# The order of the output quarters and input turns at the end of a stage

## The chip, the cores and the metric

The kernel runs on one core of a Trainium2 chip. The metric is the device time of one execution in microseconds (us); the median of three runs is 2865.96 us, with 2865.45 and 2866.62 at the ends.

## The reference

The program computes three transformer-like blocks one after the other on a residual `x` of 256 tokens x 1024 features in float32. It has ten gated feed-forward networks (width 2816), a gated delta rule, latent attention, a hybrid of a state-space model and block attention, a spatial gating unit and a pooling mixer. Cut to what matters here, each stage has this form:

```
x = x + 0.5 * ((silu(gate) * up) @ w_down)        # a feed-forward network
x = x + concat(mixed) @ w_out                     # a mixer
h = rms_norm(x, g)       or      x = layer_norm(alpha * x + ..., g, b)
```

So a stage ends with a product into the 256 x 1024 residual, and the next stage begins with that residual, turned (transposed) and normed, as input of its first product.

## The kernel before

Every product of float32 operands is made of three float32r matmuls: both operands are split in a rounded high part (`hi`, by ScalarE) and a rest (`lo`, by VectorE), and hi x hi, hi x lo and lo x hi are added in PSUM. Weights come by DMA from SyncE's queue into five slots. `load_weights` waits with `used` until TensorE has given a slot back; `round_weights` (L213) makes the high part on ScalarE, `split_weights` (L232) the rest on VectorE, at most three items ahead. Each engine works through its instructions in the order in which the program issues them, and waits on semaphores.

The output of a stage is 256 tokens x 1024 features, held in the four banks of `acc`. A quarter is 128 tokens x 512 features, one bank. `quarter` (L337) multiplies 256 rows of the weights (one item, here called a tile) into it: 2 x 3 matmuls of 512 columns. The output product goes over the rows in tiles, four quarters per tile. The last two tiles, n and n + 1, are done by `last_rows` (L353), which mixes their quarters. Quarter i of tile n + 1 completes the sum of quarter i of the output: the first three count up `quarters`, the last `used`. `before(j)` is the caller's hook ahead of the j-th step; for j = 0 and j = 2 it waits for the split of the operand of the one or the other tile (in the latent mixer, j = 1 also issues the last head's product).

When a quarter is complete, `add_quarter` (L376, on VectorE) adds it to `x` (L384 or L386). Then comes the tail of the stage, of one of two kinds:

- `FeedTail` (L523): the next stage's input is `x` as it is. `turn` (L413) transposes 128 x 512 elements by four matmuls (L421) into one of two banks of `work`; it waits for the addition of that quarter, and for turns 2 and 3 (counted from 0) also for the split of the turn two before. `round_quarter` (L431 without a gain, L436 with) runs on ScalarE, `split_quarter` (L446, L451) on VectorE. Turns 0 and 1 stand in `last_rows`, 2 and 3 in the next stage's first product (`before_chunk`, L506). VectorE's order is: additions 0 and 1, weight splits, input splits 0 and 1, additions 2 and 3, input splits 2 and 3, inverse root and diagonals (L473 to L477), weight splits. ScalarE's order is: weight rounding, input roundings 0 and 1, weight rounding, input roundings 2 and 3, squares (L463), root (L466). TensorE then sums the diagonals to a row (L491).
- `NormTail` (L566): the residual is normed first. All four turns stand in the next stage. VectorE's order is: weight splits, addition and statistics of the first two quarters, norm of the first 128 tokens (L632, L641), third addition, in the most cases the input splits 0 and 1, fourth addition, norm of the other tokens.

`last_rows` ends fourteen stages. The delta mixer (residual additions from 437 us) has its own order and does not call it.

| first addition, us | stage that ends | tail | input rounding |
|---|---|---|---|
| 223.87 | feed-forward | FeedTail | with gain |
| 626.38 | feed-forward | FeedTail | plain |
| 833.53 | feed-forward | FeedTail | plain |
| 922.23 | latent mixer | FeedTail | plain |
| 1105.13 | feed-forward | FeedTail | with gain |
| 1291.07 | feed-forward | NormTail | plain |
| 1721.71 | hybrid mixer's output | NormTail | plain |
| 1909.07 | feed-forward | NormTail | plain |
| 2095.82 | feed-forward | FeedTail | with gain |
| 2243.07 | gating mixer | FeedTail | plain |
| 2428.60 | feed-forward | FeedTail | plain |
| 2612.00 | feed-forward | FeedTail | with gain |
| 2671.50 | pooling mixer | FeedTail | plain |
| 2856.16 | feed-forward | NormTail | none, the output is stored |

Of the kernel before, what the change touches and what calls it, by code (L numbers as in the profile page):

```python
# [96 lines left out]
class Core:  # L97
# [255 lines left out]
    def last_rows(self, pe, n, pairs, tail, before):  # L353
        order = tail.order
        self.arrived(pe, n)
        for i in range(2):
            before(i)
            self.quarter(pe, n, pairs[0], order[i], False, False)
        self.arrived(pe, n + 1)
        for i in range(2):  # L360
            before(2 + i)
            self.quarter(pe, n + 1, pairs[1], order[i], False, True).then_inc(*self.quarters.up())
        before(4)
        self.quarter(pe, n, pairs[0], order[2], False, False)
        if tail.early:
            tail.feed.turn(pe, 0)
        before(5)
        self.quarter(pe, n, pairs[0], order[3], False, False).then_inc(self.used, 1)
        if tail.early:
            tail.feed.turn(pe, 1)  # L370
        before(6)
        self.quarter(pe, n + 1, pairs[1], order[2], False, True).then_inc(*self.quarters.up())
        before(7)
        self.quarter(pe, n + 1, pairs[1], order[3], False, True).then_inc(self.used, 1)

# [190 lines left out]
class NormTail:  # L566
    early = False
    order = BY_TOKENS
# [3269 lines left out]
```

## Time and profile before

| what | value |
|---|---|
| median of three runs | 2865.96 us |
| the profiled execution's own time | 2871.76 us |
| its span, first to last instruction | 2869.9 us |
| TensorE busy | 2784.2 us, 97% |
| VectorE busy | 1795.8 us, 63% |
| ScalarE busy | 1491.9 us, 52% |
| granted TensorE clock, mean | 0.994 |
| moved by DMA | 489.14 MB |

A matmul is shown with its modelled end, so neighbours overlap: the distance from one start to the next is what it costs. Idle time before an instruction is put down to the semaphore event that came last; "issue" is idle time for which the profile shows no releaser. Times in the rows count from the start of the span.

### The profile page before, as it was taken

The numbers are of one execution on the slowest core, as the hardware profiler recorded it, in microseconds if no ns is written. First come the engines' busy times: TensorE is split into PE (matmuls) and PEld (weight loads), VectorE is DVE, ScalarE is ACT, GpSimd is POOL, SyncE is SP. The second block draws the span as 40 slices with busy tenths as digits, with TensorE's granted clock in tenths as the row PEclk, the third lists the DMA queues.
The fourth block names the chain that finished last, engine by engine and source line by source line (L and its number), as shares of the span: only waits on it lengthen the run. The fifth ranks groups of instructions, "written<-read, shape, count | busy, mean of one in ns | idle before, by whom it ended". The sixth has DMA issues, their size and how long they took to land. (4 is left out here: it accounts for less than half of the span.)

```text
span 2869.9 us, 47489 instructions
## 1 busy us (share of the span) xinstructions
PE 2784.2 (97%) x20533; PEld 2599.5 (91%) x20533; DVE 1795.8 (63%) x2467; ACT 1491.9 (52%) x2011; POOL 26.5 (1%) x41
## 2 busy tenths in 40 slices
PE   7999999999999999999999999999999999999999
PEld 7998978999986999999998998989999899998898
DVE  5557756566666656555678656466656656656755
ACT  6447545455555555443575634445454555554653
POOL 1000000000000000000001000000000000000000
PEclk9999999999999999999999999999999999999999
DMA  6555115655652566665453455655565565564654
GB/s 227 191 177 163 59 45 176 191 181 180 195 165 80 186 194 207 193 191 165 144 179 104 133 175 192 192 176 191 191 191 176 167 194 192 183 195 158 198 191 132
DMA packets 370111, 489.14 MB, mean 170 GB/s; under 512 B 15424, under 2 KB 329186, under 8 KB 369776
## 3 DMA queue, kind: packets, MB, share of 16 engines
q1 hardware_dynamic: 368944, 485.90, 53.1%
q8 instruction: 162, 2.65, 0.4%
q14 instruction: 45, 0.37, 0.0%
q0 software_dynamic: 640, 0.20, 0.0%
q10 hardware_dynamic: 320, 0.01, 0.0%
HBM read 485.02 MB, written 1.05 MB: 169 GB/s over the span
## 5 line engine op out<-in xcount | busy, mean ns | idle before, releaser
L887 PE MATMUL work<-input_hi,weights_hi 128*128 128x256 f32 x3424 | 950.6, 278 | 1.9 <-DVE weights_lo L251 1.8
L889 PE MATMUL work<-input_lo,weights_hi 128*128 128x256 f32 x3424 | 947.0, 277 | 0.0
L890 PE MATMUL work<-input_hi,weights_lo 128*128 128x256 f32 x3424 | 946.7, 276 | 0.0
L241 DVE TENSOR_TENSOR weights_lo<-weights_raw,weights_hi 128x2048 fp32r<-128x2048 f32 (+2 forms) x282 | 629.4, 2235 | 321.4 <-ACT weights_hi L221 320.9
L887 PEld LDWEIGHTS work<-input_hi,weights_hi 128*128 128x128 f32 x3424 | 643.5, 188 | 3.0 <-DVE weights_lo L251 2.2
L889 PEld LDWEIGHTS work<-input_lo,weights_hi 128*128 128x128 f32 x3424 | 643.5, 188 | 0.2
L890 PEld LDWEIGHTS work<-input_hi,weights_lo 128*128 128x128 f32 x3424 | 643.1, 188 | 0.0
L225 ACT ACTIVATE weights_hi<-weights_raw,params 128x512 fp32r<-128x512 f32 (+2 forms) x736 | 462.0, 701 | 317.9 <-DMA weights_raw<-in_ffn_w_gu 157.6
L221 ACT ACTIVATE weights_hi<-weights_raw 128x2048 fp32r<-128x2048 f32 (+2 forms) x282 | 524.2, 1865 | 160.0 <-DMA weights_raw<-in_ffn_w_up 97.2
L251 DVE SCALAR_TENSOR_TENSOR weights_lo<-weights_raw,params,weights_hi 128x512 fp32r<-128x512 f32 (+2 forms) x736 | 492.4, 732 | 163.3 <-ACT weights_hi L225 163.2
L344 PE MATMUL acc<-weights_hi,hidden_hi 128*128 128x512 f32 x880 | 344.5, 392 | 2.9 <-ACT v_mla L2229 1.4
L349 PE MATMUL acc<-weights_hi,hidden_lo 128*128 128x512 f32 (+1 forms) x970 | 343.6, 370 | 0.0
L345 PE MATMUL acc<-weights_lo,hidden_hi 128*128 128x512 f32 x880 | 343.0, 390 | 0.0
L284 PE MATMUL work<-input_hi,weights_hi 128*128 128x256 f32 (+1 forms) x960 | 273.5, 285 | 4.2 <-DVE input_lo L451 2.2
L285 PE MATMUL work<-input_lo,weights_hi 128*128 128x256 f32 (+1 forms) x960 | 268.6, 280 | 0.0
L286 PE MATMUL work<-input_hi,weights_lo 128*128 128x256 f32 (+1 forms) x960 | 268.6, 280 | 0.0
L1050 DVE TENSOR_TENSOR gate_r<-work,inverse_root 128x512 f32<-128x512 f32 x97 | 66.9, 690 | 258.5 <-PE work L890 258.5
L349 PEld LDWEIGHTS acc<-weights_hi,hidden_lo 128*128 128x128 f32 x970 | 182.1, 188 | 38.5
L1006 ACT ACTIVATE hidden_hi<-hidden 128x512 fp32r<-128x512 f32 x107 | 67.6, 632 | 269.8 <-DVE hidden L1058 269.8
L344 PEld LDWEIGHTS acc<-weights_hi,hidden_hi 128*128 128x128 f32 x880 | 165.3, 188 | 34.8 <-issue 2.0
L345 PEld LDWEIGHTS acc<-weights_lo,hidden_hi 128*128 128x128 f32 x880 | 165.3, 188 | 30.4
L284 PEld LDWEIGHTS work<-input_hi,weights_hi 128*128 128x128 f32 (+1 forms) x960 | 181.3, 189 | 6.4 <-DVE input_lo L451 2.7
(565 smaller groups left out, 3471.2 us busy)
## 6 DMA issues: line engine op xcount, KB each, us to landing
weights_raw<-in_ffn_w_gu SPq DMA_DIRECT2D x176, 512.0 KB, 4.7
weights_raw<-in_ffn_w_in SPq DMA_DIRECT2D x176, 512.0 KB, 4.7
weights_raw<-in_ffn_w_down SPq DMA_DIRECT2D x66, 1024.0 KB, 4.9
weights_raw<-in_w_in SPq DMA_DIRECT2D x44, 1024.0 KB, 5.3
weights_raw<-in_ffn_w_out SPq DMA_DIRECT2D x44, 1024.0 KB, 4.9
weights_raw<-in_a_w_in SPq DMA_DIRECT2D x29, 1024.0 KB, 5.4
weights_raw<-in_ffn_w_gate SPq DMA_DIRECT2D x44, 512.0 KB, 4.0
weights_raw<-in_ffn_w_up SPq DMA_DIRECT2D x44, 512.0 KB, 5.0
```

The source lines that it names most:

```text
L221: last = self.nc.scalar.activation(self.wh[:, n % SLOTS, 0:kc * cols], raw, ACT.Copy)
L225: last = self.nc.scalar.activation(hi[:, k, :], raw[:, k * cols:(k + 1) * cols], ACT.Copy, scale=g[:, gain[1] + k:gain[1] + k + 1])
L241: last = self.nc.vector.tensor_tensor(self.wl[:, n % SLOTS, 0:kc * cols], raw, self.wh[:, n % SLOTS, 0:kc * cols].bitcast(F32), ALU.subtract)
L251: last = self.nc.vector.scalar_tensor_tensor(out=lo[:, k, :], in0=raw[:, k * cols:(k + 1) * cols], scalar=g[:, gain[1] + k:gain[1] + k + 1 ...
L284: self.nc.tensor.matmul(o, wh[:, k, ms], hi[:, k, :], start=clear, stop=False, skip_group_check=True)
L285: self.nc.tensor.matmul(o, wh[:, k, ms], lo[:, k, :], start=False, stop=False, skip_group_check=True)
L344: self.nc.tensor.matmul(o, hi[:, k, ts], wh[:, k, cols], start=(first and k == 0), stop=False, skip_group_check=True)
L345: self.nc.tensor.matmul(o, hi[:, k, ts], wl[:, k, cols], start=False, stop=False, skip_group_check=True)
L349: last = self.nc.tensor.matmul(o[:, piece.start - half * 512:piece.stop - half * 512], lo[:, k, ts], wh[:, k, piece], start=False, stop=(e ...
L887: nc.tensor.matmul(o, wh[:, k, ms], K.hi[:, c, :], start=(c == 0 and m == 0), stop=False, skip_group_check=True)
L889: nc.tensor.matmul(o, wh[:, k, ms], K.lo[:, c, :], start=False, stop=False, skip_group_check=True)
L890: last = nc.tensor.matmul(o, wl[:, k, ms], K.hi[:, c, :], start=False, stop=(c == DC - 1), skip_group_check=True)
```

## The change

In `last_rows`, the third quarter of tile n is issued ahead of the wait for tile n + 1 and of its first two quarters. The two turns each stand one quarter later: the first behind the fourth quarter of tile n, the second behind the third quarter of tile n + 1. The hooks `before(j)` keep their numbers with their quarters. Nothing else is changed.

Written as a sequence, with A for tile n, B for tile n + 1 and T for a turn: before A0 A1 B0 B1 A2 T0 A3 T1 B2 B3; after A0 A1 A2 B0 B1 A3 T0 B2 T1 B3.

```diff
--- before.py
+++ after.py
@@ -356,20 +356,20 @@
         for i in range(2):
             before(i)
             self.quarter(pe, n, pairs[0], order[i], False, False)
+        before(4)
+        self.quarter(pe, n, pairs[0], order[2], False, False)
         self.arrived(pe, n + 1)
         for i in range(2):
             before(2 + i)
             self.quarter(pe, n + 1, pairs[1], order[i], False, True).then_inc(*self.quarters.up())
-        before(4)
-        self.quarter(pe, n, pairs[0], order[2], False, False)
-        if tail.early:
-            tail.feed.turn(pe, 0)
         before(5)
         self.quarter(pe, n, pairs[0], order[3], False, False).then_inc(self.used, 1)
         if tail.early:
-            tail.feed.turn(pe, 1)
+            tail.feed.turn(pe, 0)
         before(6)
         self.quarter(pe, n + 1, pairs[1], order[2], False, True).then_inc(*self.quarters.up())
+        if tail.early:
+            tail.feed.turn(pe, 1)
         before(7)
         self.quarter(pe, n + 1, pairs[1], order[3], False, True).then_inc(self.used, 1)
```

## Rows read from the trace of the kernel before

**Rows 1.** The page's first part: engine busy time, share of span, instructions.
```profile
PE 2784.2 (97%) x20533; PEld 2599.5 (91%) x20533; DVE 1795.8 (63%) x2467; ACT 1491.9 (52%) x2011; POOL 26.5 (1%) x41
```

**Rows 2.** TensorE's waits over the span: waiter <- releaser: us, times, longest.
```profile
PE acc L491 <- DVE root_diagonals L477: 4.3, 8, 1.6
...
PE work L421 <- DVE x L386: 3.6, 3, 1.5
...
PE acc L344 <- DVE weights_lo L241: 2.9, 1, 2.9
...
PE work L421 <- issue: 1.3, 4, 0.3
...
PE acc L344 <- DVE hidden_lo L1061: 0.7, 1, 0.7
...
PE acc L344 <- DVE sgu_out_lo L3567: 0.6, 1, 0.6
```

**Rows 3.** TensorE in time at 224: start, us, operation, count, [idle before <-releaser].
```profile
222.24 0.39 PE L344 MATMUL acc<-weights_hi,hidden_hi 128*128 128x512 f32 x1
...
223.60 0.39 PE L344 MATMUL acc<-weights_hi,hidden_hi 128*128 128x512 f32 x1
...
226.33 0.60 PE L421 MATMUL work<-const,x 128*128 128x128 f32 x4
...
228.16 0.60 PE L421 MATMUL work<-const,x 128*128 128x128 f32 x4
...
231.86 0.63 PE L421 MATMUL work<-const,x 128*128 128x128 f32 x4 [0.35 <-issue]
```

**Rows 4.** VectorE in time, the same end.
```profile
223.87 0.75 DVE L384 SCALAR_TENSOR_TENSOR x<-acc,half_inverse_root,x 128x512 f32<-128x512 f32 x1 [2.03 <-PE acc L349]
225.16 0.75 DVE L384 SCALAR_TENSOR_TENSOR x<-acc,half_inverse_root,x 128x512 f32<-128x512 f32 x1 [0.54 <-PE acc L349]
225.83 2.28 DVE L241 TENSOR_TENSOR weights_lo<-weights_raw,weights_hi 128x2048 fp32r<-128x2048 f32 x1
228.15 1.13 DVE L451 SCALAR_TENSOR_TENSOR input_lo<-work,params,input_hi 128x128 fp32r<-128x128 f32 x4
229.97 1.13 DVE L451 SCALAR_TENSOR_TENSOR input_lo<-work,params,input_hi 128x128 fp32r<-128x128 f32 x4 [0.70 <-ACT input_hi L436]
231.01 1.40 DVE L384 SCALAR_TENSOR_TENSOR x<-acc,half_inverse_root,x 128x512 f32<-128x512 f32 x2
```

**Rows 5.** ScalarE in time, the same end.
```profile
228.79 1.14 ACT L436 ACTIVATE input_hi<-work,params 128x128 fp32r<-128x128 f32 x4 [0.68 <-PE work L421]
```

**Rows 6.** TensorE in time at the end at 834.
```profile
831.80 0.47 PE L344 MATMUL acc<-weights_hi,hidden_hi 128*128 128x512 f32 x1 [0.72 <-DVE hidden_lo L1061]
...
841.01 0.60 PE L421 MATMUL work<-const,x 128*128 128x128 f32 x4
```

**Rows 7.** VectorE in time, the same end.
```profile
839.86 0.74 DVE L384 SCALAR_TENSOR_TENSOR x<-acc,half_inverse_root,x 128x512 f32<-128x512 f32 x1
```

**Rows 8.** ScalarE in time at the ends at 626 and 922.
```profile
635.01 1.25 ACT L431 ACTIVATE input_hi<-work 128x512 fp32r<-128x512 f32 x2
...
930.44 0.60 ACT L431 ACTIVATE input_hi<-work 128x512 fp32r<-128x512 f32 x1 [0.16 <-PE work L421]
```

**Rows 9.** VectorE in time at the ends at 1291, 1722 and 2856.
```profile
1291.07 0.74 DVE L384 SCALAR_TENSOR_TENSOR x<-acc,half_inverse_root,x 128x512 f32<-128x512 f32 x1
...
1721.71 0.69 DVE L386 SCALAR_TENSOR_TENSOR x<-x,acc 128x512 f32<-128x512 f32 x1
...
2860.14 1.41 DVE L641 SCALAR_TENSOR_TENSOR x<-x,inverse_root,gain_rows 128x512 f32<-128x512 f32 x2
2861.53 0.75 DVE L384 SCALAR_TENSOR_TENSOR x<-acc,half_inverse_root,x 128x512 f32<-128x512 f32 x1
```

**Rows 10.** Stretches: length, engines busy (instructions), granted clock, DMA share, GB/s.
```profile
231.00:240.00 9.00, 5.21 (x39) 3.73 (x38) 5.11 (x15) 6.68 (x15) 0.00 (x0) 1.00 0.68 201
2652.00:2656.00 4.00, 4.00 (x12) 3.12 (x11) 3.16 (x7) 2.14 (x5) 0.00 (x0) 0.57 0.29 119
```

## The prediction

> **What bounds the kernel now.** I read the page's shares first: the tensor engine is busy 97% of 2869.9 us [rows 1], so only its idle time can be won or lost. The list of who waits for whom on that engine comes next [rows 2]. Two kinds of entry touch this change. One is the wait of a quarter of the last tile for the last hidden or mixed split: 0.7 us once (L1061) and 0.6 us once (L3567). The other is the wait of the turns of the next input (L421) for a residual addition: 3.6 us over three places (L386) and 1.3 us over four that the list calls "issue". After these, most stages' first sum of a row (L491) waits 4.3 us over eight places for the chain that starts with the same turns. So at the ends of stages the tensor engine arrives before vector and scalar engine are through: the ends are set by a chain on those two, and by where it starts.
>
> The chain is seen in the end at 224 us (I name an end by its first residual addition). A quarter costs 223.60 - 222.24 = 1.36 us, a turn is issued at 226.33 and the next at 228.16 [rows 3]. On the vector engine the first two additions stand at 223.87 and 225.16, each waiting for its quarter; then a weight split of 2.28 us, the split of the first turned quarter at 228.15, of the second at 229.97, and behind it, in program order, the third addition at 231.01 with no wait, though its quarter was done by then [rows 4]. The second split waits for the scalar engine's rounding at 228.79, and that for the turn at 228.16 [rows 5]. The third turn needs the third addition, and starts at 231.86 after 0.35 us idle [rows 3]. The path is: first quarter of the last tile, addition, turn, rounding, split, third addition, third turn. The quarters of the last-but-one tile that stand behind it are its cover.
>
> **The change, part by part.** Count of instructions: none is added or removed. The eight quarters keep their 48 matmuls, the turns their four transposes each; with no wait the tensor engine would leave last_rows at the same moment. No DMA is moved in the code. The slot of the last-but-one tile is given back behind the same number of quarters and one turn less, about 0.4 us earlier, so weight loads start a little sooner, which is worth nothing while no load ends a wait here.
>
> Part one: quarter three of the last-but-one tile goes ahead of the last tile. Where the last tile's operand is late it fills the wait. It gains the 0.72 us at 834 [rows 6] and 0.59 us at 2243 [rows 2]; of the second I count only 0.29, since that wait is measured from the end of a quarter two of whose matmul records are missing. A quarter that starts after a wait also costs about 0.1 us more (0.47 for its first matmul against 0.39, [rows 6, 3]). Elsewhere the operand is there in time. On the other side, the first two quarters of the last tile, and with them the first two additions, come 1.36 us later in every one of the 14 ends, less what the filled wait returns.
>
> Part two: each turn stands one quarter later. The second turn, at 228.16, goes to 229.52. Rounding, second split, third addition and third turn follow it by the same 1.36 us [rows 3 to 5]; the vector side (first addition, weight split, first split) arrives just as much later, so neither half of the change can be hidden behind the other. At the third turn the engine already waits 0.35 us, so nothing covers the shift: it idles 0.35 + 1.36 us there. What comes after it (rounding of the last quarters, squares, root, diagonals) all moves along.
>
> Price per end. Ends 224, 1105, 2096, 2612 (the input is scaled by a gain, splits of 1.13 us) already have the 0.33 to 0.35 us wait: 1.36 each, 5.4 us. End 2671 waits for the third addition already, in the 3.6 us row [rows 2], and its operand is ready: 1.36. End 2243 is of the same kind: 1.36 - 0.29 - 0.10 = 0.97.
>
> End 834: the wait gone, the first quarter of the last tile starts at 832.28 in place of 831.80, the vector chain is 0.38 later, the third addition ends at 839.86 + 0.74 + 0.38 = 840.98, and the third turn can start at 841.08 in place of 841.01 [rows 6, 7]: 0.07. Ends 626, 922 and 2429 have that slack but no wait to give back (0.06 at most). At 922 the second split ends 1.37 later, the third addition ends at about 930.54, the third turn starts near 930.64, 0.83 later than now. At 626 the turn itself would be 0.56 late, but the rounding of the third quarter already stands without a wait behind weight rounding [rows 8], which begins behind the second turn's rounding, and moves by 1.0. At 2429 the slack is as at 922 (there the rounding waits 0.16 us for its turn [rows 8]) and the filled wait returns a little: 0.60. Each of them has its 0.3 us wait at the row sum, so all of it arrives there: 0.83 + 1.0 + 0.60 = 2.4 us.
>
> Ends with a layer norm have no turns inside. At 1291 the first addition stands without a wait behind a weight split [rows 9]; its quarter, moved to 1290.9, is still in time, and so at 1909: 0 each. At 1722 the addition waits for its quarter, and the norm chain moves 1.05 (its root is late by 0.3 for another reason now, which the shift hides); the turns had been free of wait, the splits behind them come 0.71 later: 0.71. The last end, 2856: after the two scalings that end at 2861.55 comes the third addition at 2861.53 [rows 9]. The scalings move by 1.37; the third addition, which meets its quarter exactly, and all behind it up to the store, by 1.32.
>
> Sum: 5.4 + 1.36 + 0.97 + 0.07 + 2.4 + 0.71 + 1.32 = 12.3 us more idle tensor time.
>
> One cost is not seen before: the idle stretch at 2243 and 2671 grows from 1.5 to 2.5 and 2.9 us. The nearest row is the 2.9 us wait for a weight split [rows 2]; the stretch 2652 to 2656 behind it has a granted clock of 0.57 [rows 10], 4.0 x 0.43 = 1.7 us of work lost at the lower level. On the other side 231 to 240 was busy 5.21 of 9.00 us and kept 1.00 [rows 10]. So between 0 and 3.4 us for the two ends; I take one fall, 1.7, as one of them is near 2.9 and one nearer 2.5. [...]
>
> The profiled execution took 2871.76 us, its span and 1.9 us around it, 5.8 above the median of 2865.96. The sum of differences, 14.0, would bring it to 2885.8; on the median it gives 2880.0 us.
>
> **The rivals.** First, on the other side: the filled waits are all that counts. If the third turn is not tied to the second split (its wait is called "issue", and at 834, 922 it is not waited for at all), the vector chain has spare time of a quarter, the tensor engine keeps its own order, and gains the 0.72 and 0.29 us, some 0.1 us each at 626 and 2429, and the restarts at four places (0.4): 1.6 to 2.0 us, 2864. It decides where the third addition would end before the engine is ready, that is, where the slack at the third turn is over 1.36 us. Against it: the slack at the third turn is nought at six of the ten ends with turns, and at the other four under 1 us.
>
> Second: the shift is felt only where a wait is named for an addition: 2243, 2671, 1722, 2856, that is 0.97 + 1.36 + 0.71 + 1.32 = 4.4 us, 2870.4; elsewhere the chain's own spare time takes it. For it: the other waits are 0.35 us or none. Against: the row sums wait at eight places [rows 2].
>
> Third: the clock falls at more ends. At the ends with a gain the engine would idle 1.7 us at the third turn, besides the waits that follow within ten. If four of those and the two above each lose 1.7 us: 12.3 + 10.2 = 22.5, 2888. Against: 231 to 240 [rows 10].
>
> **How the numbers follow.** My forecast 0.77, first rival 0.06, second 0.09, third 0.08. A change of under 0.2% (5.7 us) is about what a measurement of this kernel can't tell from none. Faster by more needs something outside the cases: 0.02. Within it lie both the first and second rival: 0.13 after a little for the outside. Slower 0.85. My own terms give 12.3 without a fall and 15.7 with two, and errors of a few tenths at each of ten ends; with a part of the third rival and the upper end of the second the range is 2872 to 2884.
>
> **What would show it.** In the changed profile: at 224, 1105, 2096, 2612 the wait of the third turn near 1.7 us; at 2671 near 2.9; the 0.7 us for L1061 and the 0.6 for L3567 gone; the third additions 1.36 later after the last-but-one tile's start, 0.4 at 834; no change at 1291 and 1909; the end from the last matmul to the last scaling 1.3 longer. Wrong would be: third turns without longer waits, or row sums whose wait shrinks by what the turns lost.

## The result, and the profile after

The changed kernel takes 2879.93 us (median of four runs, 2877.39 to 2882.52), the kernel before 2866.11 us beside it: ratio 1.005, 95% interval 1.0038 to 1.0063. A second measurement on another occasion gave 2880.64 against 2866.9 us, ratio 1.0049, interval 1.0034 to 1.0063. The change costs 13.8 us in the first measurement and 13.7 us in the second, 0.5%; 2880.0 us was forecast.

First the page of the changed kernel, its first part, which answers to [rows 1]:

```profile
PE 2781.1 (97%) x20533; PEld 2596.5 (90%) x20533; DVE 1794.9 (62%) x2467; ACT 1491.6 (52%) x2011; POOL 26.5 (1%) x41
```

The counts are the same and no engine is busier. The time is idle time. The two profiled executions differ by less than the medians (spans of 2869.9 and 2877.8 us): the one of before took 2871.76 us, 5.8 above its median, the changed one 2879.7, and the difference lies mostly in the start-up, below. TensorE's waits over the span of the changed kernel (waiter, releaser, us, times, longest), against [rows 2]:

```profile
PE work L421 <- issue: 9.8, 8, 1.7
PE work L421 <- DVE x L386: 6.3, 3, 2.9
...
PE acc L344 <- DVE weights_lo L241: 4.1, 2, 2.9
PE acc L491 <- DVE root_diagonals L477: 4.0, 6, 1.6
```

The turns' waits went from 1.3 to 9.8 us and from 3.6 to 6.3 us, 11.2 together. The waits for the hidden split (0.7 us, L1061) and the gating unit's split (0.6 us, L3567) are gone. The row sum's wait hardly changed (4.3 to 4.0 us): it did not give back what the turns lost. These balance to 9.6 us; the longer tail behind the last matmul, below, is 1.3 more, and a wait at 1722, told further down, 0.3.

The end at 224 stands at 220 in this execution because of its start-up, which has nothing to do with the change: a wait at some 45 us was 2.46 us (L284, 3.91 before), and the granted clock from 40 to 60 us was 1.00 (0.83 before, 3.4 us of work). TensorE in time, its three turns, against [rows 3]:

```profile
222.62 0.60 PE L421 MATMUL work<-const,x 128*128 128x128 f32 x4
...
224.44 0.60 PE L421 MATMUL work<-const,x 128*128 128x128 f32 x4
...
228.13 0.63 PE L421 MATMUL work<-const,x 128*128 128x128 f32 x4 [1.70 <-issue]
```

VectorE in time, the same end, against [rows 4]:

```profile
220.16 0.75 DVE L384 SCALAR_TENSOR_TENSOR x<-acc,half_inverse_root,x 128x512 f32<-128x512 f32 x1 [3.39 <-PE acc L349]
221.45 0.75 DVE L384 SCALAR_TENSOR_TENSOR x<-acc,half_inverse_root,x 128x512 f32<-128x512 f32 x1 [0.54 <-PE acc L349]
222.12 2.28 DVE L241 TENSOR_TENSOR weights_lo<-weights_raw,weights_hi 128x2048 fp32r<-128x2048 f32 x1
224.43 1.13 DVE L451 SCALAR_TENSOR_TENSOR input_lo<-work,params,input_hi 128x128 fp32r<-128x128 f32 x4
226.25 1.13 DVE L451 SCALAR_TENSOR_TENSOR input_lo<-work,params,input_hi 128x128 fp32r<-128x128 f32 x4 [0.69 <-ACT input_hi L436]
227.29 1.40 DVE L384 SCALAR_TENSOR_TENSOR x<-acc,half_inverse_root,x 128x512 f32<-128x512 f32 x2
```

The wait ahead of the first addition grew from 2.03 to 3.39 us, one quarter of 1.36. From the first addition on every distance is that of before: to the second split 6.09 against 6.10 us, to the third addition 7.13 against 7.14. So the whole chain moved as one piece, and TensorE, whose quarters end where they did, waits 1.70 us in place of 0.35. The label "issue" is the same wait for the third addition: the turn starts 0.84 us after that addition does, here as in [rows 3, 4] (0.85).

The end at 834, TensorE and then VectorE in time, against [rows 6, 7]:

```profile
839.75 0.63 PE L421 MATMUL work<-const,x 128*128 128x128 f32 x4 [0.89 <-issue]
```

```profile
838.91 1.40 DVE L384 SCALAR_TENSOR_TENSOR x<-acc,half_inverse_root,x 128x512 f32<-128x512 f32 x2
```

No matmul waits for the hidden split any more, and TensorE is some 0.8 us earlier at the third turn, where it waits 0.89 us. The filled wait came back one step later.

VectorE in time at the last end, against [rows 9]: the hidden split, the scalings of the first tokens, the third addition, and the last scalings:

```profile
2860.03 0.69 DVE L1061 TENSOR_TENSOR hidden_lo<-hidden,hidden_hi 128x512 fp32r<-128x512 f32 x1 [0.70 <-ACT hidden_hi L1006]
...
2868.11 1.41 DVE L641 SCALAR_TENSOR_TENSOR x<-x,inverse_root,gain_rows 128x512 f32<-128x512 f32 x2
2869.44 0.74 DVE L384 SCALAR_TENSOR_TENSOR x<-acc,half_inverse_root,x 128x512 f32<-128x512 f32 x1
...
2873.35 1.42 DVE L641 SCALAR_TENSOR_TENSOR x<-x,inverse_root,gain_rows 128x512 f32<-128x512 f32 x2
```

and the same two ends of that stretch in the kernel before:

```profile
2853.43 0.69 DVE L1061 TENSOR_TENSOR hidden_lo<-hidden,hidden_hi 128x512 fp32r<-128x512 f32 x1 [0.70 <-ACT hidden_hi L1006]
...
2865.44 1.42 DVE L641 SCALAR_TENSOR_TENSOR x<-x,inverse_root,gain_rows 128x512 f32<-128x512 f32 x2
```

From the hidden split's start to the last scaling's end it was 13.43 us and is 14.74: 1.3 longer.

And at 1291 (here 1292.61), the first addition still stands without a wait behind its weight split, and what follows is unchanged:

```profile
1292.61 0.74 DVE L384 SCALAR_TENSOR_TENSOR x<-acc,half_inverse_root,x 128x512 f32<-128x512 f32 x1
```

### The profile page after: what moved, and what is told of

It is laid out like the page before. It is cut to its first block and busy times, and to the rows that moved or that the text cites. A ratio compares the mean times of both kernels' runs of the same rounds, so it can differ in the third digit from the quotient of the medians.

```text
span 2877.8 us, 47489 instructions
## 1 busy us (share of the span) xinstructions
PE 2781.1 (97%) x20533; PEld 2596.5 (90%) x20533; DVE 1794.9 (62%) x2467; ACT 1491.6 (52%) x2011; POOL 26.5 (1%) x41
## 5 line engine op out<-in xcount | busy, mean ns | idle before, releaser
L241 DVE TENSOR_TENSOR weights_lo<-weights_raw,weights_hi 128x2048 fp32r<-128x2048 f32 (+2 forms) x282 | 629.4, 2235 | 312.7 <-ACT weights_hi L221 312.1
L284 PE MATMUL work<-input_hi,weights_hi 128*128 128x256 f32 (+1 forms) x960 | 272.7, 284 | 4.2 <-DVE input_lo L451 2.2
L284 PEld LDWEIGHTS work<-input_hi,weights_hi 128*128 128x128 f32 (+1 forms) x960 | 180.5, 188 | 6.3 <-DVE input_lo L451 2.7
```

The costliest lines, as they stand in the source:

```text
L241: last = self.nc.vector.tensor_tensor(self.wl[:, n % SLOTS, 0:kc * cols], raw, self.wh[:, n % SLOTS, 0:kc * cols].bitcast(F32), ALU.subtract)
L284: self.nc.tensor.matmul(o, wh[:, k, ms], hi[:, k, :], start=clear, stop=False, skip_group_check=True)
```

## The experiments

All start from the kernel before, or where it is said from the changed one. The edits are shown shortened; "..." marks what is left out. A, B and T in the orders are those of the section on the change. Added or moved lines shift the line numbers behind them by two or more, so L421 is L423 in most of these profiles.

**The third quarter alone.** The turns keep their place behind the fifth and sixth quarter.

```diff
+        before(4)
+        self.quarter(pe, n, pairs[0], order[2], False, False)
         self.arrived(pe, n + 1)
         ...
-        before(4)
-        self.quarter(pe, n, pairs[0], order[2], False, False)
         if tail.early:
             tail.feed.turn(pe, 0)
```

> Only the third quarter of the last-but-one tile is brought forward; the turns stay behind the fifth and the sixth quarter (A0 A1 A2 B0 B1 T0 A3 T1 B2 B3). Theory (the chain turn, rounding, second split, third addition, third turn sets the ends, and the vector engine's additions, weight split and first split are its second leg): the scalar leg doesn't move, the vector leg moves by 1.36 us. At 224, 1105, 2096, 2612 the third addition comes about 0.5 us later, at 2671 1.36, at 2243 0.97, at 626, 922, 2429 0.2 to 0.5, at 834 nothing, at 1722 0.7 and at 2856 1.3: 7 us, about 2873. Rival (only the place of the turns costs, the third quarter is free or a gain): 2864 to 2866, third turns at 224 and its like with the wait of 0.35 us as before.

Measured: 2875.9 us against 2866.52, ratio 1.0035, interval 1.0022 to 1.0047. TensorE's second and third turn in the first such end, and VectorE in the same end, in time:

```profile
226.04 0.60 PE L423 MATMUL work<-const,x 128*128 128x128 f32 x4
230.19 0.63 PE L423 MATMUL work<-const,x 128*128 128x128 f32 x4 [0.78 <-issue]
```

```profile
223.12 0.75 DVE L386 SCALAR_TENSOR_TENSOR x<-acc,half_inverse_root,x 128x512 f32<-128x512 f32 x1 [3.39 <-PE acc L349]
...
225.08 2.28 DVE L241 TENSOR_TENSOR weights_lo<-weights_raw,weights_hi 128x2048 fp32r<-128x2048 f32 x1
227.28 2.15 DVE L453 SCALAR_TENSOR_TENSOR input_lo<-work,params,input_hi 128x128 fp32r<-128x128 f32 x8
229.35 1.40 DVE L386 SCALAR_TENSOR_TENSOR x<-acc,half_inverse_root,x 128x512 f32<-128x512 f32 x2
```

The addition comes 1.36 us late, but the two splits now run as one block of 2.15 us: the second, whose rounding is in time, no longer waits for it (0.70 us before). So VectorE alone is what holds the third addition, 0.43 us later than before (0.78 against 0.35 us of wait). The rival, that the third quarter is free, falls. At 2243 and 2671 the wait is 2.9 us, as in the full change. The kernel lost 9.4 us where 7 were expected. The waits of the trace and the longer tail make 6.5 us; the mean granted clock is 0.9934 in these ten executions and 0.9943 in the 33 beside them, which is 2.6 us more.

**The turns later, alone.** (A0 A1 B0 B1 A2 A3 T0 B2 T1 B3.)

```diff
         self.quarter(pe, n, pairs[0], order[2], False, False)
-        if tail.early:
-            tail.feed.turn(pe, 0)
         before(5)
         self.quarter(pe, n, pairs[0], order[3], False, False).then_inc(self.used, 1)
+        if tail.early:
+            tail.feed.turn(pe, 0)
         ...
```

> Only the turns stand one quarter later (A0 A1 B0 B1 A2 A3 T0 B2 T1 B3). Theory: at the four ends with a gain the third turn comes 1.36 us later; at 626, 834, 922, 2429 0.9 to 1.4; at 2243 and 2671 nothing, because there the vector engine is in its weight split of 5.4 us; at the ends with a layer norm nothing. Sum 9.7 us, about 2876. The wait for the last hidden split at 834 (0.7 us) stays. Rival (only the third quarter costs): 2866 and the waits at the third turn as before.

Measured: 2875.84 us, ratio 1.0036, interval 1.0025 to 1.0047. TensorE's waits over the span:

```profile
PE work L423 <- issue: 9.6, 8, 1.7
...
PE work L423 <- DVE x L388: 3.6, 3, 1.5
...
PE acc L344 <- DVE sgu_out_lo L3569: 0.6, 1, 0.6
PE acc L344 <- DVE hidden_lo L1063: 0.6, 1, 0.6
```

Eight places with 9.6 us, near the 9.8 of the full change, but 3.6 us for the additions at 2243 and 2671, as before: there the weight split of 5.4 us covers the later turn. The time is as expected, 9.3 us. Each edit alone costs some 9.4 us, 19 in sum, both together 13.7. The intervals of these times are some 3 us to either side, but the waits say the same: at 224 the third turn's wait grows by 0.43 us with the one edit, by 1.35 with the other and by 1.35 with both. The two edits move two legs of one chain, of which the later one counts.

**The turns earlier.**

```diff
             self.quarter(pe, n + 1, pairs[1], order[i], False, True).then_inc(*self.quarters.up())
+        if tail.early:
+            tail.feed.turn(pe, 0)
         before(4)
         self.quarter(pe, n, pairs[0], order[2], False, False)
         if tail.early:
-            tail.feed.turn(pe, 0)
+            tail.feed.turn(pe, 1)
```

> The mirror of the change's second part: the order of before with each turn one quarter earlier (A0 A1 B0 B1 T0 A2 T1 A3 B2 B3). Theory: at the ends with a gain the second split is through before the third addition's own quarter is, the 0.35 us wait of the third turn goes and about 0.4 us is won at each; at 626, 922, 2429 0.3 us of the row sum's wait; at 2243 and 2671 nothing (the weight split of 5.4 us holds the vector engine). About 2.5 us faster, 2863.5. Rival (the turns' place has slack on this side: the chain is bound by the first additions): no change, 2866, and the 0.35 us waits stay. Second rival: a turn right behind the last tile's second quarter waits itself for its addition, +0.1 to 0.3 us at each of ten ends, 2868.

Measured: 2863.1 us, ratio 0.9986, interval 0.9976 to 0.9997. That is 3.4 us faster, 2.5 were expected. No turn has an "issue" wait, which gives 1.3 us; the 0.3 us waits at the row sums of 626, 922 and 2429, which were expected to go, stayed at 0.32 to 0.33 us. The third turn in the first end:

```profile
226.87 0.60 PE L423 MATMUL work<-const,x 128*128 128x128 f32 x4
```

VectorE in time, the same end:

```profile
223.55 2.15 DVE L453 SCALAR_TENSOR_TENSOR input_lo<-work,params,input_hi 128x128 fp32r<-128x128 f32 x8
225.71 0.75 DVE L386 SCALAR_TENSOR_TENSOR x<-acc,half_inverse_root,x 128x512 f32<-128x512 f32 x1
```

The second split is done 6.3 us after the first addition, and the third addition starts at once, about when its quarter is complete, too. The place of the turns matters in both directions. With the third addition at its quarter, a further gain would need an earlier quarter, not an earlier turn (reasoned, not run).

**And the weight items split apart**, on top of the earlier turns.

```diff
-        K.split_weights(dve, K.taken + 2)
+        two = K.n_split <= K.taken
+        K.split_weights(dve, K.taken + (1 if two else 2))
         feed.split_quarter(dve, 0)
         feed.split_quarter(dve, 1)
         for i in range(2, 4):
             K.add_quarter(dve, i, self.order[i], self.quarter_at, last_item, alpha, scale_of)
+        K.split_weights(dve, K.taken + 2)
```

> As the run with earlier turns, and at the two ends where two weight items are still to be split (2243, 2671) the second of them is split behind the fourth addition instead of ahead of the first input split. Theory: the vector leg there loses 2.7 us, the third turn's wait of 1.5 us goes at both, 3 us less than with earlier turns alone, about 2860.5. Rival (the weight item is then late for the next stage): the wait moves from the third turn to the first matmuls of the second item, no gain, 2863.5.

Measured: 2860.05 us, ratio 0.9977, interval 0.9967 to 0.9987. VectorE in time at the end of the gating mixer:

```profile
2239.29 2.73 DVE L251 SCALAR_TENSOR_TENSOR weights_lo<-weights_raw,params,weights_hi 128x512 fp32r<-128x512 f32 x4
2241.94 1.28 DVE L448 TENSOR_TENSOR input_lo<-work,input_hi 128x512 fp32r<-128x512 f32 x2
2243.71 0.69 DVE L388 SCALAR_TENSOR_TENSOR x<-x,acc 128x512 f32<-128x512 f32 x1 [0.48 <-PE acc L349]
2245.07 0.69 DVE L388 SCALAR_TENSOR_TENSOR x<-x,acc 128x512 f32<-128x512 f32 x1 [0.68 <-PE acc L349]
2245.68 2.73 DVE L251 SCALAR_TENSOR_TENSOR weights_lo<-weights_raw,params,weights_hi 128x512 fp32r<-128x512 f32 x4
```

The two items of 2.73 us stand on either side of the additions, which now wait for their quarters, and TensorE's wait for an addition falls from 3.6 us to the 0.5 us of the delta mixer's end, which none of these edits touches. The moved item makes no new wait. The time is 3.0 us below that with the earlier turns alone, where 3 were expected.

**The changed kernel with the third addition ahead of the second split.**

```diff
         feed.split_quarter(dve, 0)
+        K.add_quarter(dve, 2, self.order[2], self.quarter_at, last_item, alpha, scale_of)
         feed.split_quarter(dve, 1)
-        for i in range(2, 4):
-            K.add_quarter(dve, i, self.order[i], self.quarter_at, last_item, alpha, scale_of)
+        K.add_quarter(dve, 3, self.order[3], self.quarter_at, last_item, alpha, scale_of)
```

> The changed kernel, with the third addition put ahead of the second input split on the vector engine in the ends without a norm; tensor and scalar engine as in the change. Theory (the third turn is late because its addition stands behind the second split in the queue): the third turn at 224, 1105, 2096, 2612 starts without a wait of note (1.7 us now), but the fourth turn waits some 0.6 us for the second split, so about 0.7 us is won at each; at 2243 and 2671 the 2.9 us wait becomes 2.2; at 626, 834, 922, 2429 the 0.7 us waits go and 0.2 to 0.5 is won. Sum 4 to 5 us, about 2875. Rival (the third turn waits for something else that moved with the turns, such as the bank or the scalar engine): the 1.7 us waits stay, 2880.

Measured: 2874.18 us, ratio to the kernel before 1.0026, interval 1.0016 to 1.0035. TensorE in time, the third turn and the first matmul that waits behind it, in the first end:

```profile
226.90 0.63 PE L423 MATMUL work<-const,x 128*128 128x128 f32 x4
...
228.11 0.28 PE L284 MATMUL work<-input_hi,weights_hi 128*12 128x256 f32 x1 [0.59 <-DVE input_lo L453]
```

The 1.7 us wait of the turn is gone with nothing changed but the order of two steps on VectorE (an addition and a split), so it was the queue position behind the second split that made it. The 0.6 us that was expected at the fourth turn is there, but at the next stage's first matmul: it needs the second split, too (`before_chunk` awaits both token halves), and comes sooner. At 2243 and 2671 2.3 us are left, 2.2 expected; at 626, 922 and 2429 the third turn no longer waits, at 834 it still waits 0.29 us. At the four ends with a gain 1.1 us each is won, not 0.7: a wait of 1.7 us became one of 0.6. At 626 nearly nothing is won, since the row sum waits 1.27 us in place of 0.59. In all 6 us are won where 4 to 5 were expected.

**The weight split of the ends with a norm, later**, on top of the earlier turns and the split items.

```diff
-        K.split_weights(dve, K.taken + 2)
         add(0, 0)
         add(0, 1)
         norm(0)
         add(1, 0)
         if self.first_tokens:
             split(0)
+        K.split_weights(dve, K.taken + 2)
```

> As the run with earlier turns and the weight items split apart, and in the ends with a norm the weight split stands behind the first two input splits, not ahead of the first addition. Theory: at 1291 the norm chain starts 1.4 us earlier and the first product of the next stage with it, the 1.97 us wait becomes 0.6; at 1909 the first half gains 2.4 us, and the second gives most of it back (its turns then wait for a chain that carries the weight split of 2.7 us), 0.2 net; at 1722 and 2856 there is no item left to split. 1.6 us less than with the two edits alone, about 2858.5. Rival (the next stage needs that weight item earlier than its new place): waits for a weight split appear at the start of both stages, 2861 to 2864.

Measured: 2859.0 us, ratio 0.9975, interval 0.9966 to 0.9984. Beside 0.9977 this can't be told from the run without it. At 1291 the two turns run without a wait, and the first product behind them, TensorE in time:

```profile
1298.26 1.03 PE L423 MATMUL work<-const,x 128*128 128x128 f32 x8
1300.91 0.36 PE L2670 MATMUL work<-weights_hi,input_hi 128*128 128x256 f32 x1 [1.62 <-DVE input_lo L448]
```

1.62 us in place of 1.97, not 0.6. I had left out that the turns themselves can't start before the last quarter ends; behind them stands a turn, a rounding and a split in a row. The chain was 1.4 us earlier, but only 0.24 + 0.35 us of it could be had. At 1909 the waits add up to 2.9 us against 3.4.

**The third quarter in the ends with a norm only.** The changed order where `tail.early` is false, the old one elsewhere (a sketch, not the code; the steps are those of the section on the change).

```diff
+        if not tail.early:
+            (A0 A1 A2 B0 B1 A3 B2 B3)
+        else:
+            (A0 A1 B0 B1 A2 T0 A3 T1 B2 B3)
```

> Before, with the third quarter brought forward only in the four ends with a norm (A0 A1 A2 B0 B1 A3 B2 B3 there, the old order and old turns elsewhere). Theory: 0 at 1291 and 1909, 0.7 at 1722, 1.3 at 2856, 2 us in all, about 2868.5; the trace of the last end is 1.3 longer from the last hidden split to the last scaling. Rival (these ends have cover everywhere, as the additions can catch up under the last quarters): 2866.5 and an unchanged last end.

Measured: 2869.89 us, ratio 1.0014, interval 1.0003 to 1.0024. VectorE in time, last end, from the hidden split to the last scaling:

```profile
2852.62 0.69 DVE L1082 TENSOR_TENSOR hidden_lo<-hidden,hidden_hi 128x512 fp32r<-128x512 f32 x1 [0.70 <-ACT hidden_hi L1027]
2856.70 0.75 DVE L405 SCALAR_TENSOR_TENSOR x<-acc,half_inverse_root,x 128x512 f32<-128x512 f32 x1 [3.39 <-PE acc L349]
...
2865.93 1.41 DVE L662 SCALAR_TENSOR_TENSOR x<-x,inverse_root,gain_rows 128x512 f32<-128x512 f32 x2
```

From 2852.62 to 2867.34 that is 14.72 us, against 13.43 in the kernel before: 1.29 longer, and the same 1.3 as in the full change. The rival, that the additions catch up, falls. The time is 3.0 us longer where 2 were expected, which the interval allows.

**The changed kernel again.**

> The changed kernel once more, on the chip and beside the runs of the next three. Theory: 12.3 us of idle time over before, plus what the clock adds, 2878 to 2880. If the first measurement was carried by clock falls, it is 2872 to 2875.

Measured as told at the top, 2880.64 us. Its eight "issue" waits are 9.8 us and its three for an addition 6.3 us, to the tenth those of the first profile. The expectation's other case, 2872 to 2875 us if clock falls had carried the first measurement, did not come.

## Why the prediction was right

The place of the loss, point by point. The third turn at 224, 1105, 2096 and 2612: about 1.7 us forecast, 1.70, 1.71, 1.71 and 1.71 us read in the changed profile, 1.35 to 1.38 more each. At 2671: 2.9 forecast and read. At 834 the third turn's wait came with no net gain. At 1291 and 1909 nothing moved. The tail of the last end: 1.32 forecast, 1.3 read. That both edits move two legs of one chain is shown by the runs with one edit each, and that the link is the queue on VectorE by the run with two of its steps swapped.

Sizes that were off. At 2243 the wait is 2.90 us, not 2.5: TensorE arrives 0.39 us earlier (filled wait and restart), and I had not added this to the idle stretch, though the net of 0.97 holds it. The ends without a gain together: waits at the third turn and the row sum rose from 0.32 to 1.31 us at 626, 0.31 to 0.99 at 922, 0.32 to 1.06 at 2429, so 1.0, 0.7 and 0.7 where 1.0, 0.83 and 0.60 were forecast. At 834 the waits for the hidden split, at the third turn and at the row sum rose from 1.04 to 1.22 in sum, 0.18 for 0.07. At 1722 the first product's wait is 1.26 for 0.98 us: 0.28 for 0.71. But the kernel before does not stay at 0.98 there: the run with only the turns later, whose order in that end is the old one, has 1.26 too, because there the root on ScalarE is behind a weight rounding that had waited 4.65 us for its weights. In the second changed profile the turns of that end wait 0.37 us besides the 1.26. So that end's term was put on a base which moves by itself.

The sum of idle time by these waits is 11.3 us for 12.3: 5.3 at the four ends with a gain, 1.4 at 2671, 0.6 at 834 and 2243 together (the row sum's 0.32 us at 2243 being given back), 2.4 at 626, 922 and 2429, 0.3 at 1722, 1.3 at the end. The rest of the 13.7 us, 2.4, is in part the clock, below. I had taken 1.7 for it. So the idle time was forecast 1.0 us too high and the rest 0.7 too low: that the forecast met the median to 0.1 us is luck, while the places and most of the sizes are not.

The first rival (TensorE gains the filled waits) is excluded by the result and by the run with the third quarter alone. The second (only the places named for an addition pay) by the 9.8 us of "issue". The third (the clock falls at six ends) did not come.

**The clock.** In the 10 us behind the third turn at 2243 and 2671, stretches of the changed kernel (length, engines, granted clock next to last but two):

```profile
2254.00:2264.00 10.00, 9.97 (x71) 9.95 (x72) 5.22 (x10) 6.08 (x11) 0.00 (x0) 0.83 0.19 64
2686.00:2696.00 10.00, 9.94 (x74) 9.91 (x75) 5.26 (x10) 5.20 (x11) 0.00 (x0) 0.86 0.35 132
```

and of the run with the third quarter alone, which has the same two waits of 2.9 us (it kept 1.00):

```profile
2252.80:2262.80 10.00, 9.62 (x81) 9.41 (x82) 5.25 (x10) 7.19 (x13) 0.00 (x0) 1.00 0.35 117
2682.00:2692.00 10.00, 9.43 (x81) 9.40 (x82) 5.76 (x11) 5.99 (x12) 0.00 (x0) 1.00 0.49 181
```

Behind a wait of 2.9 us the clock fell to its lower level, 1.2 GHz, in four of six cases (the changed kernel twice, both ends each time; not in this run), behind 2.3 us in both cases (the run with the third addition ahead), behind 1.5 us in none of eight (four profiles, the kernel before among them), with no wait in none of four (the two runs with the weight items split apart). A fall is 1.4 to 1.7 us less work (0.17 and 0.14 of 10 us; 0.29 once, where it stayed low for twice as long). So the term of one fall was of the right size, and which execution has it is open.

A third turn's wait of 1.7 us stands at the ends with a gain in twelve places: four in each changed profile and four in the run with only the turns later. The clock fell behind one of them, at 2108 in the first changed profile. The run with the third quarter alone has the same fall (0.83 from 2107 to 2117), though its third turn waits only 0.79 us there; both have a wait of 1.8 us for a split just before it (1.80 us in the kernel before, too, which kept its clock). Nor does the length of a wait alone decide: behind one of 1.97 us at 1299, which the change leaves as it is, the clock fell in eight of nine profiles (0.83 from 1299 to 1309 in the kernel before), and the one without a fall is the first changed profile (1.00 from 1301 to 1311).

The Trainium skill, "TensorE: Matmul & The Clock Gate", section "HAM oscillation — how this bites in real kernels", has a kernel whose array starts cold again after the wait between two bursts of matmuls; the waits of its example are longer than any at these turns. The traces agree with it for the waits of 2.3 and 2.9 us, six falls in eight cases, and not for those of 1.7 us, one in twelve.

What stays open: 13.7 less 11.3 is 2.4 us. The mean granted clock of the executions is 0.9942 in the 29 of the kernel before and 0.9937 in the six of the changed one beside them; 0.0005 of 2880 us is some 1.5 us, a rough figure with six executions. What remains is below what these runs can tell.

## What to carry to other kernels

When operations are reordered to fill a wait on the busiest engine, ask first which chain starts with the ones that move back. Here waits of 0.7 and 0.6 us at two places were filled, and the quarter that starts the residual chain moved back at all fourteen. The busiest engine only hides a chain if it has work behind the chain's start: move the start forward and leave the filler behind it. And when an engine works through its steps in program order, two independent chains on it become one: swapping one addition with one split was worth 6 us on the changed kernel, without touching the engine that had waited.

The version with earlier turns and the weight items split apart beats both kernels, 0.9977 of the kernel before; with the norm ends' weight split moved it is 0.9975, which is not separate from it.

## What was not expected

- A wait of 1.21 us for a weight split (L241) stands at 2664 in the changed profile and not in that of before. It is not the change's: the runs with only the turns later, and with the turns earlier, have it as well (two such waits, 4.1 and 4.0 us, for one of 2.9), while the two experiments whose clock fell at 2644 and 2655 have not, as the kernel before, whose clock fell at 2652 [rows 10]. So it goes in all ten profiles. The likely reason, which no run isolates, is that the weights catch up while the clock is low; the fall would then cost little there.
- Executions of one kernel spread over 10 us or more (the kernel before from 2859.11 to 2873.96 us in 33 runs), and the mean granted clock goes with it: 0.996 or 0.997 in the six fastest, 0.992 to 0.994 in all over 2867 us. In the other set of 29 it holds with exceptions (two over 2867 us have 0.995 and 0.996). With ten to twelve executions against some thirty the interval is about 3 us to either side; the waits at the turns, which repeat to 0.02 us from profile to profile, tell more.
